# Expert rows gathered in four quarters and turned by VectorE instead of TensorE

## The reference, cut to what matters

```python
scores = sigmoid(xt @ w_router)                       # 64 experts
_, idx = top_k(scores + router_bias, 6)               # 6 experts for each token
gate   = scores[idx] / sum(scores[idx]) * 2.5
# token-slots sorted by expert, each expert's rows padded to whole blocks of 128
def run_block(tok, g, e):
    return swiglu(x_pad[tok], w_exp_gu[e], w_exp_down[e]) * g[:, None]
routed = zeros(T + 1, D).at[row_tok].add(out)
# D_MODEL = 1024, D_EXPERT = 256, all float32
```

## Time and the profile before

| | |
|---|---|
| median of 3 runs | 2167.43 us (2162.13 to 2168.65) |
| profiled execution | 2157.31 us, span 2155.4 us |
| granted clock, mean over the span | 0.975 of full |
| TensorE matmul busy | 2044.7 us, 95% of the span |
| VectorE, ScalarE, GpSimd busy | 870.4, 611.1, 412.1 us |
| bytes moved by DMA | 365.07 MB |
| expert loop | from about 1319 to about 2098 us of the span |

### The profile page before, as it was taken

How to read it: one execution, slowest core, us unless ns; L and a number is a source line. 1 busy time by engine, 2 the same in 40 slices (tenths; PEclk the granted TensorE clock), 3 DMA queues, 4 the chain that set the end, 5 groups by cost and what they waited for, 6 DMA issues and landing times.

```text
span 2155.4 us, 24298 instructions
## 1 busy us (share of the span) xinstructions
PE 2044.7 (95%) x8206; PEld 1148.6 (53%) x8206; DVE 870.4 (40%) x2352; ACT 611.1 (28%) x1204; POOL 412.1 (19%) x581
## 2 busy tenths in 40 slices
PE   8999999999999999998999997999999999999990
PEld 6666645666655665565455453544454454444440
DVE  4373365999765451150455641111111111111116
ACT  2223554662566540030223000111111111111112
POOL 0031000010220001101222251222222222222224
PEclk9999999999999999999999998999999999999995
DMA  5040113110110011134221404999999999999994
GB/s 183 3 42 8 42 34 123 40 48 2 25 27 1 2 45 44 29 103 130 108 68 49 156 40 150 367 362 366 371 368 362 374 367 364 365 372 364 361 337 175
DMA packets 127155, 365.07 MB, mean 169 GB/s; under 512 B 31329, under 2 KB 79202, under 8 KB 109282
## 3 DMA queue, kind: packets, MB, share of 16 engines
q1 hardware_dynamic: 105250, 289.80, 36.2%
q0 software_dynamic: 20016, 72.88, 13.3%
q10 hardware_dynamic: 1808, 1.33, 0.2%
HBM read 310.82 MB, written 53.04 MB: 169 GB/s over the span
## 4 chain that ended last, share of the span: by engine, by line
PE 89%; DMA 3%; ACT 3%; DVE 3%; issue 1%; POOL 0%; SPq 0%; POOLq 0%; DVEq 0%; ACTq 0%
PE psum L878 21%; PE psum L603 11%; PE psum L892 11%; PE psum L744 8%; PE psum L762 6%; PE psum L618 4%; PE psum L471 3%; ACT arena L1300 3%; PE psum L870 3%; PE psum L425 3%; PE psum L815 3%; PE psum L679 2%; PE psum L460 2%; PE psum L698 2%; PE psum L665 2%; PE psum L806 2%
## 5 line engine op out<-in xcount | busy, mean ns | idle before, releaser
L1300 ACT ACTIVATE arena<-psum 128x512 f32<-128x512 f32 (+9 forms) x709 | 326.7, 497 | 1260.2 <-PE psum L878 445.1
L878 PE MATMUL psum<-arena 128*128 128x512 f32 x1088 | 480.3, 594 | 1.1 <-DVE arena L2218 1.1
L878 PEld LDWEIGHTS psum<-arena 128*128 128x128 f32 x1088 | 202.7, 191 | 230.5 <-issue 229.3
L892 PE MATMUL psum<-arena 128*128 128x512 f32 x544 | 244.8, 593 | 0.5 <-ACT arena L1300 0.5
L603 PE MATMUL psum<-arena 128*128 128x384 f32 (+1 forms) x768 | 239.6, 471 | 0.1
L2223 DVE TENSOR_TENSOR arena<-arena,psum 128x256 f32<-128x256 f32 x68 | 28.6, 421 | 454.6 <-ACT arena L1300 454.6
L603 PEld LDWEIGHTS psum<-arena 128*128 128x128 f32 x768 | 144.2, 190 | 95.4 <-issue 11.4
L744 PE MATMUL psum<-arena 128*128 128x384 f32 (+1 forms) x576 | 178.6, 473 | 5.8 <-DMA arena<-in_w_attn_proj 5.8
L1259 POOL TENSOR_TENSOR carry<-ones 1x1 f32<-1x1 f32 x135 | 52.0, 385 | 568.2 <-DVE arena L2232 520.9
L1848 DVE TENSOR_SCALAR_CACHE_REDUCE arena<-arena 128x512 uint8<-128x512 f32 (+6 forms) x175 | 154.8, 929 | 2.0
L892 PEld LDWEIGHTS psum<-arena 128*128 128x128 f32 x544 | 98.4, 191 | 98.7 <-issue 98.0
(11 more groups left out here) (302 smaller groups left out, 2283.3 us busy)
## 6 DMA issues: line engine op xcount, KB each, us to landing
arena<-in_w_exp_gu SPq DMA_DIRECT2D x69, 2048.0 KB, 8.9
arena<-in_w_exp_down SPq DMA_DIRECT2D x68, 1024.0 KB, 7.6
arena<-in_w_in SPq DMA_DIRECT2D x24, 512.0 KB, 4.5
arena<-in_x_prompt SPq DMA_DIRECT2D x10, 512.0 KB, 4.2
arena<-in_w_glu SPq DMA_DIRECT2D x16, 256.0 KB, 4.9
arena<-in_w_attn_proj SPq DMA_DIRECT2D x16, 256.0 KB, 4.6
arena<-in_w_out SPq DMA_DIRECT2D x1, 4096.0 KB, 13.0
x_d<-arena SPq DMA_DIRECT2D x8, 512.0 KB, 2.9
```

The lines of the kernel that those rows point to most:

```text
L878: last = mm(psum[:, 2, :], xgT[u][:, k, :], ewg[u][:, k, :], start=k == 0, stop=k == DK - 1)
L892: last = mm(psum[:, 4 + 2 * u + j, :], ehT[u][:, k, :], ewd[u][:, k, j * 512:(j + 1) * 512], start=k == 0, stop=k == 1)
L1300: return act.activation(dst, src, fn, **kw)
```

## The change

It moves the turning of the gathered rows from TensorE (and the copies out of PSUM) to VectorE. VectorE can turn squares of 32 x 32. For that the rows have to lie differently: the gather is cut into four indirect DMAs, g = 0 to 3, each of which brings to partition 32a+i the a-th quarter (256 features, 1 KB) of the token in slot 32g+i. For that the token list has four columns, with entries 4*token+a, which are made ahead of the loop by four more matmuls that spread the table's rows, and one VectorE operation on their product.

```diff
-        xg = [at(0, DM), at(1024, DM)]
+        xg = [at(0, 4, 2 * P), at(1024, 4, 2 * P)]
...
-        tid = [sb(f"tid{u}", [P, 1], I32) for u in range(2)]
+        tid = [sb(f"tid{u}", [P, 4], I32) for u in range(2)]
+        piece = sb("piece", [P, 2])
+        tab4, spread = at(46080, 4, NBP), at(46592, 4, 4, 32)
...
# TensorE, ahead of the loop, before the last shared_down
+                    if i == NT:
+                        pe.wait_ge(s("tab_ready"), 2)
+                        b = claim("tab4", "tab_ready", 3, pool=SIX)
+                        for g in range(4):
+                            last = mm(psum[:, b, g * NBP:(g + 1) * NBP],
+                                      spread[:, g, :, :].rearrange("p a i -> p (a i)"),
+                                      tab[:, 0, :], start=True, stop=True)
+                        filled(last, "tab4")
                     shared_down(i - 1)
...
# TensorE, in the loop
-            def turn_rows(u, loads):
-                pe.wait_ge(s(f"xg_loaded{u}"), loads)
-                for half in range(2):
-                    for q in range(4):
-                        last = tr(psum[:, half, q * P:(q + 1) * P], xg[u][:, 4 * half + q::DK], ident[:])
-                    last.then_inc(s(f"xg_turned{half}"), 1)
...
-                pe.wait_ge(s("xgT_ready"), blocks * 2)
+                pe.wait_ge(s("xgT_ready"), blocks)
...
                     gate_and_up(1 - u, n + 2, ip * 16 + 16 + 16 * u)
-                    turn_rows(u, ip * 16 + 32)
                     down(u, n + 1, ip * 16 + 16)
...
# GpSimd
             def gather(u):
-                pool.indirect_dma_start(xg[u], None, x1_d,
-                                        bass.IndirectOffsetOnAxis(ap=tid[u][:, 0:1], axis=0)
-                                        ).then_inc(s(f"xg_loaded{u}"), 16)
+                for g in range(4):
+                    pool.indirect_dma_start(xg[u][:, g, :], None, x1_d.rearrange("t (a f) -> (t a) f", a=4),
+                                            bass.IndirectOffsetOnAxis(ap=tid[u][:, g:g + 1], axis=0)
+                                            ).then_inc(s(f"xg_loaded{u}"), 16)
...
# ScalarE, in the loop
-            def half_rows(u, blocks):
-                act.wait_ge(s("xg_turned0"), blocks)
-                f(xgT[u][:, 0:4, :], psum[:, 0, :].rearrange("p (q n) -> p q n", q=4)).then_inc(s("xgT_ready"), 1)
...
# VectorE, ahead of the loop, in the pass i == NT - 1
-                    step(stt(tab[:, 0, :], tab[:, 0, :], -1.0, empty, ALU.add, ALU.add))
-                    list_rows(0, tab[:, 0, 0:1])
-                    list_rows(1, tab[:, 0, 1:2])
+                    stt(tab[:, 0, :], tab[:, 0, :], -1.0, empty, ALU.add, ALU.add).then_inc(s("tab_ready"), 1)
+                    dve.wait_ge(s("tab_ready"), 2)
+                    await_bank(dve, "tab4")
+                    ts(tab4[:].rearrange("p g n -> p (g n)"), bank("tab4")[:, 0:4 * NBP], 4.0, piece[:, 0:1], ALU.mult,
+                       ALU.add).then_inc(s("tab_ready"), 1)
+                    dve.wait_ge(s("tab_ready"), 3)
+                    list_rows(0, slice(0, 1))
+                    list_rows(1, slice(1, 2))
...
# VectorE, in the loop
-            def half_rows(u, blocks):
-                dve.wait_ge(s("xg_turned1"), blocks)
-                dve.tensor_copy(xgT[u][:, 4:8, :], psum[:, 1, :].rearrange("p (q n) -> p q n", q=4)
-                                ).then_inc(s("xgT_ready"), 1)
+            def turn_rows(u, loads):
+                dve.wait_ge(s(f"xg_loaded{u}"), loads)
+                for g in range(4):
+                    last = dve.transpose(xgT[u][:, :, 32 * g:32 * g + 32],
+                                         xg[u][:, g, :].rearrange("p (j k) -> p k j", k=DK))
+                last.then_inc(s("xgT_ready"), 1)
...
-                    list_rows(1 - u, tab[:, 0, bass.ds(n + 3, 1)])
+                    list_rows(1 - u, bass.ds(n + 3, 1))
                     gate_up(1 - u, n + 2)
-                    half_rows(u, n + 3)
+                    turn_rows(u, ip * 64 + 128)
                     half_y(u, n, n + 1, ip * 16 + 16)
```

More of the change, by code:

```diff
@@ L896, in _ @@
             pe.wait_ge(s("base_ready"), NT)
-            turn_rows(0, 16)
             gate_and_up(0, 1, 16)
-            turn_rows(1, 16)
             turn_eh(0, 1)
@@ L1145, in _ @@
             pool.memset(zlag, 0.0).then_inc(s("constants"), 1)
+            step(pool.memset(piece[:], 0.0))
+            for a in range(1, 4):
+                step(pool.memset(piece[32 * a:32 * a + 32, :], float(a)))
             pool.memset(carry[:], 0.0).then_inc(s("constants"), 1)
@@ L1577, in _ @@
             act.wait_ge(s("tab_ready"), 1)
-            half_rows(0, 1)
             silu(0, 1)
-            half_rows(1, 2)
             take_eh(0, 1)
@@ L2179, in list_rows @@
             def list_rows(u, column):
-                ts(tid[u][:], column, 1.0, None, ALU.mult).then_inc(s("tid_ready"), 1)
+                ts(tid[u][:], tab4[:, :, column].rearrange("p g n -> p (g n)"), 1.0, None,
+                   ALU.mult).then_inc(s("tid_ready"), 1)
+            for a in range(4):
+                last = dve.tensor_copy(spread[:, :, a, :], ident[:].rearrange("p (g i) -> p g i", i=32))
+            step(last)
             dve.wait_ge(s("x1_stored"), 16 * NT)
@@ L2233, in half_y @@
                    ALU.mult).then_inc(s("y_half"), 1)
-            half_rows(0, 1)
-            list_rows(0, tab[:, 0, 2:3])
+            turn_rows(0, 64)
+            list_rows(0, slice(2, 3))
             gate_up(0, 1)
-            half_rows(1, 2)
+            turn_rows(1, 64)
             with dve.Fori(0, last_pair) as ip:
```

## The result

The changed kernel takes 2150.62 us (median of 4 runs, 2146.95 to 2152.93); the kernel before, timed beside it, 2167.02 (4 runs). The ratio is 0.9926, 95% interval 0.9904 to 0.9949: faster by 0.5 to 1.0%. I had forecast 2173 us, a little slower. The time lies inside the stated range and on the side to which I had given 0.22.

A forecast was written before the change was run, and what follows sets the result against it. TensorE set the pace, with DMA engines some 98% full just behind; after the change TensorE waits for DMA. Loop +5.4, room -5, way in +5 make +5.4 us on 2167.43: 2173 us, range 2146 to 2210.

The forecast's parts named there:

- the side to which I had given 0.22: Whole kernel: a time faster by over 0.3%; chance 0.22.
- TensorE's 60.5 us: Loop: TensorE loses eight transposes, 0.89 us a block; 60.5 us over 68 blocks if nothing else held.
- the term of the DMA engines: Loop: 512 packets of 1 KB replace 128 of 4 KB; 11.24 + 0.26 = 11.50 us a block, +5.4 us.
- Rival 2: Loop: packets were priced too high, blocks take 11.02 to 11.24 us, time 2140 to 2155 us; chance 0.20.
- The 5 us of room: First blocks: TensorE runs ahead until the 2 MB load's spare landing time is used up, once; -5 us.
- The way into the loop: Ahead of the loop: four pieces +4.17, VectorE's transposes -1.0, spreading matmuls +0.9, clock +0.9; together +5 us.
- VectorE: Loop: four transposes at 0.42, 1.68 us a block, hidden in 2.62 us of room.
- GpSimd: Loop: four indirect DMAs instead of one, 4.17 us more; queue busy 7.8 of 11.4 us, not setting the pace.
- Rivals 3: Loop: TensorE still sets the pace at 10.53 us a block, 2112 us; chance 0.04.
- 4: Loop: pieces are dear, each costing as two of 512 B; 11.94 us a block, +35, 2203 us; chance 0.22.
- 6: Loop: VectorE's transposes take over 0.85 us each; at 1.2 us, 12.8 us a block, about 2266 us; chance 0.04.
- rival 5: Loop: gathers arrive late, pieces waiting for weight packets; 1.2 us a block, +82, about 2250 us; chance 0.08.

The follow-up runs named there:

- gu_7of8: The changed kernel, loading only seven eighths of the gate-and-up weights from block 2 on (output not the reference's); 2114.57 us, ratio 0.9799.
- tensor_refill: The changed kernel with eight idle transposes of the identity on TensorE in each block, where the row transposes stood; 2165.82 us, ratio 1.0033.
- before_extra: The kernel before with one more load in each block, 1 KB to each partition, that no computing engine waits for; 2162.66 us, ratio 1.0007.
- one_gather: The changed kernel with one gather of 4 KB rows in place of four of 1 KB pieces (output not the reference's); 2146.57 us, ratio 0.9954.
- half_turns: The changed kernel with VectorE making two of the four transposes of a block (output not the reference's); 2157.64 us, ratio 0.9979.

## Why the prediction was wrong

**Right: the place and the mechanism.** After the change TensorE waits for DMA, VectorE's transposes and GpSimd's four issues are hidden, and most of TensorE's 60.5 us doesn't arrive. gu_7of8 and tensor_refill show both limits, and before_extra beside one_gather shows how far apart they were in the kernel before. The wait that ends last is the gather's landing, which the DMA queues stretch.

**Wrong: the term of the DMA engines, by size.** The step said 11.24 + 0.26 = 11.50 us a block, against 11.21 measured (11.42 before). It is two errors, 0.19 us and 0.10. With 11.14 + 0.07 us the DMA work lies under the 11.42 of before and not over it, so the block lost 0.21 us where I had added 0.08.

*The piece.* I priced 1 KB at 0.0486 us, 32 of them 1.55 against 1.29 for the gather. No run measures a plain packet of 1 KB by itself: the extra load's 128, by the rows 0.37 us for each engine and block, added 0.33 and 0.44 us with the chain of the waits in it. But the pieces of the gather don't travel so. The q0 row of the changed kernel's stretch with the first three gathers, 1317 to 1336 us, that is 1536 pieces:

```profile
DMA packets 577, 1.58 MB, mean 83 GB/s; under 512 B 192, under 2 KB 192, under 8 KB 576
...
q0 software_dynamic: 576, 1.57, 28.1%
```

192 are the tiny packets of completions; the other 384 carry 1.57 MB, 4 KB each. Four pieces go as one packet, at nearly the price of a row. The same row of the kernel before, 1318.5 to 1328 us, where one whole gather is alone:

```profile
q0 software_dynamic: 144, 0.52, 17.5%
```

17.5% of 16 x 9.5 us over 128 rows are 0.208 us each, and 28.1% of 16 x 19 over 384 are 0.222: 0.11 us more for an engine's eight, 3 x 16 more completion packets for each gather among it. The lower bound that I had written down, a quarter of a 4 KB packet, was nearly right: one_gather puts what pieces cost at 0.07 us a block. The Trainium skill, DMA: Bandwidth & Descriptors, section SWDGE vs HWDGE vs iDMA, says that a packet built by GpSimd is preferably up to 4096 bytes and may hold up to 64 descriptors; the trace agrees. I had looked at the section on sizes only.

*The sum before.* The prediction took 11.24 of 11.42 us as full. With one gather, and so with the same packets as before, the DMA-bound block takes 11.14. The shares above 100% in the earlier trace rows say that durations overlap, and in the sum I treated them as work. Rival 2 had both parts. That its range, 2140 to 2155, holds the result is in part luck: it leaves out the longer way into the loop and starts from the first median, which lies 5 to 6 us high. Its block, 11.02 to 11.24, does hold the 11.21. I gave it 0.20 because I let the durations of 512 B packets speak for gathers, of which they said nothing.

**The 5 us of room** did not show in the changed kernel. Blocks 3 to 5 did start 10.53 to 10.63 us apart, TensorE's own pace. But the second block starts 12.48 after the first, where it was 10.81 before, and the first ten together take 112.0 us by the timeline, the later average already. The timeline of the changed kernel shows the first part of it:

```profile
1326.58 9.30 PE L881 MATMUL psum<-arena 128*128 128x512 f32 x16 [14.65 <-issue]
...
1336.39 0.42 DVE L2232 TENSOR_TENSOR arena<-arena,psum 128x256 f32<-128x256 f32 x1 [9.86 <-ACT arena L1305]
...
1336.73 2.19 DVE L2226 STREAM_TRANSPOSE arena<-arena 128x256 f32<-128x256 f32 x4
...
1339.06 6.27 PE L881 MATMUL psum<-arena 128*128 128x512 f32 x14 [1.68 <-DVE arena L2226]
```

Here the gather is there in time. The transposes of block 1 stand on VectorE behind the multiply of block 0, and TensorE has no `down` yet to fill the time: 1.68 us. I had looked for the room of 2.62 us only in the loop's own order, where `down` lies between.

That isn't all, for one_gather has the same 1.68 us and still takes 10.5 to 10.6 us a block from its second to its eighth; its first ten take 3.2 us less than ten later ones. The changed kernel waits from the sixth block on, behind the gather. The prediction gave the last piece 12.5 us to land, "room of nearly 5 us, if landing doesn't grow". It grew, from 8.1 in this loop before to 11.7 from the last piece's issue to VectorE, and with the later issue that was the room.

**The way into the loop**: forecast +5, measured +3.3. The first gather starts 1.7 us later, the spreading matmuls (1.1 us) before it. Its last piece is issued 3.9 us after its first but lands 2.7 us later, where the whole gather took 4.6. From landing to the first `gate_and_up` it is 2.3 us instead of 2.7. The clock's part, forecast at +0.9, is 0.2 and lies in the loop's first block: the first `gate_and_up` takes 9.30 instead of 9.06, its first 4 us at half the clock (granted 0.50) in both kernels.

**VectorE**: four transposes at 0.42 were forecast as 1.68, they take 2.2; inside the room of 2.62 us, and half_turns shows that it costs nothing.

**GpSimd**: pieces were forecast 1.39 us apart. In the loop they are 1.25 to 1.30 apart (1622.92, 1624.22, 1625.47).

Rivals 3, 4 and 6 did not come. Of rival 5 half did: the gathers do arrive last, VectorE waits for them, and the result and the scatter stand behind it as it said. But the landing grows as the end of a queue of work: with one gather the block is almost the same. Its price of 1.2 us a block did not come.

## What to carry to other kernels

When TensorE and the DMA engines are both near full, taking work off TensorE is worth the difference between the two, so that difference has to be measured: an extra load, put into the old kernel, shows it if the landing times are watched over the whole loop (here about 0.3 us a block, where the share of 1.02 had said none). No queue that matters may wait for that load, or the test makes a chain of its own. The price of small DMA pieces depends on who builds them: take it from packet counts and sizes of the same kind of DMA, not from another kind's durations. A wait that ends last on one DMA is no proof of a latency chain: shorten the chain and see whether the landing grows. And leaving out DMA rows paid here only after they were dealt out over the partitions.

## What was not expected of the hardware

- A share of 1.02 to 1.03 of the DMA engines is no proof that they are full: the kernel before took 3% more bytes at the same pace over one loop, from 367 GB/s to 378, its landing times growing meanwhile.
- Four pieces of 1 KB that GpSimd gathers go as one packet of 4 KB (384 packets for 1536 pieces), while plain loads of 1 KB to a partition go one by one (about 128 packets more under 2 KB in each block of before_extra).
- Left-out rows of an indirect DMA saved nothing when they fell to the last slots (11.25 us a block) and 0.47 us a block more when dealt out (10.78), at the same bytes. The packet count stayed: small packets take their place.
- A 4 KB packet of the scatter with addition takes 0.328 us of an engine, one of a plain load 0.161. How much of that is the addition isn't shown.
